# Attention of a hybrid encoder step: the order of 72 heads, and which query tile is prepared when

## The chip, the cores and the metric
The kernel runs on one core of one Trainium2 chip. The metric is the device time of one execution in microseconds (us). A core has five engines: TensorE (PE in the profile, with its weight loads as PEld), VectorE (DVE), ScalarE (ACT), GpSimd (POOL) and SyncE (SP), which here issues DMAs. Each runs its own program in its written order, and they meet through semaphores.

## The reference
One inference step of a one-layer encoder: a gated DeltaNet branch and an MLA attention branch over 1024 prompt rows and 32 sample rows (with 256 cached ones). What concerns the change is the attention, eight heads of 128 (plus 64 rotary) dimensions:

```python
s = einsum('bqhd,bkhd->bhqk', qn, kn) + einsum('bqhd,bkd->bhqk', qr, kr)
s = s.astype(float32) * (QK_HEAD ** -0.5)
mask = (kpos[None, :] // CHUNK) <= (qpos[:, None] // CHUNK)   # CHUNK = 64
s = where(mask, s, -inf)
pr = softmax(s, axis=-1)
return einsum('bhqk,bkhd->bqhd', pr, v)                       # per block of 128 queries
```

qn and qr are the two parts of the projected q, each divided by its root mean square; qr is then rotated by its position. The result, times silu(z_b), goes on to the output projection.

## The kernel before
The kernel has five stages with a meeting of all engines between them (`meet`): the input projections, the latents (keys and values), the attention, the delta rule, and the output branches. The attention is written as one program for each engine, which all loop over the same step number x.

There are nine query tiles of 128 rows: tiles 0 to 7 of the prompt and tile 8, the sample (`NT` is 8). Tile i of the prompt attends 128(i+1) keys, the sample 288. Each has 8 heads, so there are 72 heads, and before the change head x is head x % 8 of tile x // 8. In step x:
- TensorE (`pe_attention`): scores of head x+1 (matmuls at L695 to L697, 512 keys at a time), early jobs, values of head x-1 (L720), transposes of the probabilities of head x (L708), late jobs.
- VectorE (`dve_attention`): maximum of x+1 (`dve_max`, L930 to L934: mask, maximum, scaled and negated), after each fourth head the normalised result `on` (L946, L950), early jobs, the copy of the transposed probabilities beyond 512 keys (L959), late jobs, a step of the decay gate (`dve_decay`) where one is due, a part of the norms of q where one is due.
- ScalarE (`act_attention`): exp of x+1 (L798), early jobs, the copy pT of the first 512 keys of transposed probabilities of x (L814), late jobs, a step of the decay gate.

So every engine is one head ahead with the score side and one behind with the value side. Scores of odd and even heads use two pairs of PSUM banks; there is one bank pair for transposes, one bank for values, and one bank, number 7, for all jobs.

A job is four small transposes through bank 7 (`pe_job`, L681), read by one other engine. The dictionary `jobs` maps a step and a phase (early, late) to its jobs; `order` numbers them, and a job on TensorE waits until all earlier ones were read (`s_r7`). The kinds:
- q, parts 0 to 2: the raw q of a tile (`qraw`, one DMA) turned to rows; ScalarE reads it twice, into `qtok` and squared into `qsq` (L784, L785).
- b, parts 0 and 1: the normalised q turned back, read by ScalarE into `qT` (L787); parts 2 and 3: the rotated part, read by VectorE into `qrT` (L913).
- o: the attended group of four heads turned, multiplied by `zb` into `ub` on VectorE (L922), from where SP stores it.
- d: two jobs of the decay gate for the next stage.

Between q and b lie the norms on VectorE (`dve_q_norms`: part 0 sums and scales, L846 to L850; part 1 the inverse root, eleven small operations at L87 to L98; part 2 the multiply, L858) and the rotation on GpSimd (`pool_attention`, L829 to L839). During the 8 heads of tile i the kernel so prepares tile i+1: norms in its steps 1, 2, 3, b jobs in steps 4, 5, 6, 6, the q jobs of the tile after that in steps 6, 7 and 0 of the next. `qT` and `qrT` have two slots.

SP's program (`sp_attention`) is a single line: q loads, stores of `ub`, loads of `zb`, and, once the prompt's heads are through, the first loads of the delta stage (`sp_load_qkv`, `sp_load_gcum`), whose buffers lie where the attention's keys and values were.

Of the kernel before, what the change touches and what calls it, by code (L numbers as in the profile page):

```python
# [21 lines left out]
P = 128  # L22
# [86 lines left out]
def build(nc, a, o, scr, ctx):  # L109
# [127 lines left out]
    qT = sb(p2b, "qT", [P, 2, H, P])  # L237
    qrT = sb(p2b, "qrT", [P, 2, H, P], F32R)
# [364 lines left out]
    turn = {job: n for n, job in enumerate(order)}  # L603

# [4 lines left out]

    second = [0]  # L610
    for x in range(NX):
        second.append(second[-1] + (len(keys_of(x // H)[2]) > 4))

    def scores_of(x):
        b = 2 * (x % 2)
        return PS[:, b:b + 2].rearrange("p a b -> p (a b)")[:, 0:keys_of(x // H)[1]]

    def load_q(sp, i):
        sp.dma_start(qraw[:, :], scr["proj"][C_Q:C_Q + 12, :, i * P:(i + 1) * P].rearrange("c p n -> p c n")).then_inc(s_qraw, 16)

    def sp_attention(sp):
# [3 lines left out]
        for i in range(NQ):  # L625
            if i == NT - 1:
                sp.wait_ge(s_gT, 1)
                sp.dma_start(scr["gcum"].rearrange("t h n -> (t h) n"), gcT).then_inc(s_so, 16)
            if i + 1 < NQ:
                sp.wait_ge(s_t7, turn[("q", i, 2)] + 1)  # L630
                load_q(sp, i + 1)
            for g in range(2):
                if i:
                    sp.wait_ge(s_r7, turn[("o", 2 * i - 2 + g, 0)] + 1)
                    store_ub(sp, 2 * i - 2 + g)
                sp.dma_start(zb[:, g], scr["proj"][C_ZB + 4 * g:C_ZB + 4 * g + 4, :, i * P:(i + 1) * P].rearrange("c p n -> p c n")).then_inc(s_zb[g], 16)
        sp.wait_ge(s_pv, NT * H)
        sp.wait_ge(s_so, 16)
        for t in range(2):
            sp_load_qkv(sp, t)  # L640
            sp_load_gcum(sp, t)
        for g in range(2):
            sp.wait_ge(s_r7, turn[("o", 2 * NT + g, 0)] + 1)
            store_ub(sp, 2 * NT + g)
        for g in range(2):
            sp.wait_ge(s_us[g], 16 * NQ)

    def store_ub(sp, og):
        i, g = divmod(og, 2)
        sp.dma_start(scr["u"][H + 4 * g:H + 4 * g + 4, :, i * P:(i + 1) * P].rearrange("c p n -> p c n"), ub[:, g]).then_inc(s_us[g], 16)  # L650
# [60 lines left out]
    def pe_values(pe, x):  # L711
        i, h = divmod(x, H)
# [6 lines left out]
        for k, w in enumerate(widths):  # L719
            last = pe.matmul(PS[:, 6, (h % 4) * P:(h % 4 + 1) * P], pT[0:w, x % 2, k], V[0:w, base // P + k, h * HD:(h + 1) * HD],  # L720
# [41 lines left out]
    def act_job(act, job):  # L762
# [23 lines left out]
        else:  # L786
            act.activation(qT[:, i % 2, 4 * part:4 * part + 4].rearrange("p a b -> p (a b)"), PS[:, 7], ACT.Copy, scale=colB[:, B_QN:B_QN + 1]).then_inc(s_r7, 1)  # L787
# [3 lines left out]
    def act_exp(act, x):  # L791
        n = keys_of(x // H)[1]
# [8 lines left out]
    def act_attention(act):  # L801
# [3 lines left out]
        for x in range(NX):  # L805
# [4 lines left out]
            nk = min(4, len(keys_of(x // H)[2]))  # L810
# [9 lines left out]
    def pool_attention(pool):  # L820
        half = ROPE // 2
        for i in range(NQ):
# [4 lines left out]
            cos = rotq[:, i:i + 1, 0].to_broadcast([P, H, ROPE])  # L827
            sin = rotq[:, i:i + 1, 1].to_broadcast([P, H, ROPE])
# [76 lines left out]
    def dve_job(dve, job):  # L905
# [30 lines left out]
    def dve_attention(dve):  # L936
# [3 lines left out]
        for x in range(NX + 2):  # L940
# [12 lines left out]
            if x < NX:  # L953
                nk = len(keys_of(x // H)[2])
# [9 lines left out]
            if 1 <= x % H <= 3 and x // H + 1 < NQ:  # L964
                dve_q_norms(dve, x // H + 1, x % H - 1)
# [125 lines left out]
    def bank(g, b):  # L1091
        return PS[:, 4 * g + b]
# [1240 lines left out]
```

## Time and profile before
| | us |
|---|---|
| median of three runs | 2135.45 (2130.41 to 2136.23) |
| profiled execution | 2133.29, its span 2131.6 |
| of it: TensorE busy | 1984.1 |
| first scores to last transposes of the attention | 294.5 (1173.96 to 1468.50) |

The profile's times count from the start of the span. Busy time of TensorE is that of its matmuls, which overlap each other a little in their pipeline, so that the interval from the start of one group to the start of the next is the better measure of what a group costs. "Idle before" names the operation whose semaphore ended a wait.

### The profile page before, as it was taken

What the parts mean: (1) busy time and instruction counts of PE and PEld (TensorE: products, weight loads), DVE (VectorE), ACT (ScalarE), POOL (GpSimd) and SP (SyncE); (2) the same over time, 40 slices, a digit from 0 to 9 for tenths busy, and PEclk for the clock granted to TensorE, in tenths of its full rate; (3) what the DMA queues carried; (4) which work ended last, traced back from release to release, by engine and by line L of the source; (5) the groups of instructions that cost most, each with busy time, mean ns of one, the idle gap of its engine ahead of it and who ended that gap; (6) DMA issues with size and microseconds to landing.
All of it is one profiled execution on the core that took longest, in us unless ns stands there. A gap on an engine that the chain in (4) does not pass through costs nothing.

```text
span 2131.6 us, 32185 instructions
## 1 busy us (share of the span) xinstructions
PE 1984.1 (93%) x12375; PEld 1818.7 (85%) x12375; DVE 864.0 (41%) x1840; ACT 699.4 (33%) x1528; POOL 199.7 (9%) x248
## 2 busy tenths in 40 slices
PE   6899999999999999987986788998999998999999
PEld 2699999999999999975764567876999997799887
DVE  1545545100100010025642556655676767423332
ACT  2333333211111222213222445434667675211010
POOL 0012212000000000000001221211111010000000
PEclk9899999999999999999998899999999999999999
DMA  9122222322222222132111221115013224523231
GB/s 322 63 95 103 95 95 85 133 95 84 97 112 84 95 99 99 50 101 89 39 29 34 60 70 46 50 30 168 20 62 106 75 79 150 200 74 109 89 115 69
DMA packets 153725, 195.63 MB, mean 92 GB/s; under 512 B 9153, under 2 KB 124910, under 8 KB 153628
## 3 DMA queue, kind: packets, MB, share of 16 engines
q1 hardware_dynamic: 142300, 151.85, 21.1%
q0 software_dynamic: 10064, 38.13, 5.3%
q10 hardware_dynamic: 1264, 4.39, 0.5%
q8 instruction: 57, 0.93, 0.2%
q14 instruction: 40, 0.33, 0.1%
HBM read 134.15 MB, written 60.19 MB: 91 GB/s over the span
## 4 chain that ended last, share of the span: by engine, by line
PE 79%; DVE 8%; ACT 4%; issue 4%; DMA 3%; DVEq 1%; ACTq 0%; POOL 0%; POOLq 0%; SPq 0%
PE PS L2158 40%; PE PS L1468 9%; PE PS L1301 8%; PE PS L1400 4%; PE PS L1473 3%; PE PS L381 3%; PE PS L720 2%; PE PS L695 2%; PE PS L2174 1%; PE PS L681 1%; PE PS L708 1%; DMA Wraw<-in_w_ada 1%; ACT E L1645 1%; DVE amx L932 1%; DVE lst L530 1%
## 5 line engine op out<-in xcount | busy, mean ns | idle before, releaser
L2158 PE MATMUL PS<-HH,WL 128*128 128x352 f32 (+1 forms) x1752 | 379.8, 325 | 5.2 <-DVE mod L2268 5.2
L2158 PE MATMUL PS<-HH,WH 128*128 128x352 f32 (+1 forms) x1752 | 378.4, 323 | 0.0
L2158 PE MATMUL PS<-HL,WH 128*128 128x352 f32 (+1 forms) x1752 | 378.0, 324 | 0.0
L2158 PEld LDWEIGHTS PS<-HH,WL 128*128 128x128 f32 (+1 forms) x1752 | 298.8, 189 | 5.6 <-issue 5.3
L2158 PEld LDWEIGHTS PS<-HH,WH 128*128 128x128 f32 (+1 forms) x1752 | 301.1, 188 | 0.3
L2158 PEld LDWEIGHTS PS<-HL,WH 128*128 128x128 f32 (+1 forms) x1752 | 297.8, 188 | 0.2
L2264 DVE TENSOR_TENSOR WL<-Wraw,WH 128x2048 fp32r<-128x2048 f32 x37 | 84.8, 2293 | 523.1 <-ACT WH L2101 523.1
L2129 ACT ACTIVATE R<-PS 128x1056 f32<-128x1056 f32 x48 | 50.6, 1054 | 409.1 <-PE PS L2158 409.1
L1468 PE MATMUL PS<-WT,QL 128*128 128x128 f32 x832 | 102.5, 277 | 1.2 <-DVE QL L1858 0.9
L720 PE MATMUL PS<-V,pT 128*128 128x128 f32 (+1 forms) x624 | 86.4, 282 | 15.5 <-ACT pT L814 15.3
L1468 PEld LDWEIGHTS PS<-WT,QL 128*128 128x128 f32 x832 | 97.6, 193 | 2.6 <-DVE QL L1858 2.6
L2285 DVE SCALAR_TENSOR_TENSOR R<-R 128x1059 f32<-128x1059 f32 x72 | 95.3, 1323 | 5.4
L720 PEld LDWEIGHTS PS<-V,pT 128*128 128x128 f32 (+1 forms) x624 | 78.0, 193 | 21.5 <-ACT pT L814 19.4
L798 ACT ACTIVATE pr<-PS,amx 128x128 f32<-128x128 f32 (+8 forms) x72 | 51.5, 716 | 135.3 <-DVE amx L934 135.1
L1695 ACT ACTIVATE WT<-PS 128x512 f32<-128x512 f32 x104 | 62.1, 598 | 96.5 <-PE PS L1468 96.5
L381 PE MATMUL PS<-UH,LL 128*128 128x512 f32 x176 | 72.8, 413 | 17.0 <-DVE UL L560 11.0
L695 PE MATMUL PS<-kT,qT 128*128 128x512 f32 (+4 forms) x208 | 85.1, 492 | 1.0 <-DVEq L915 1.0
L1301 PE MATMUL PS<-FH,VL 128*128 128x352 f32 x384 | 84.3, 327 | 0.4 <-DVE FL L1271 0.4
L1301 PE MATMUL PS<-FH,VH 128*128 128x352 f32 x384 | 82.8, 323 | 0.0
L1301 PE MATMUL PS<-FL,VH 128*128 128x352 f32 x384 | 82.6, 323 | 0.0
L1998 POOL DMA_DIRECT2D Wraw<-in_w_in x36 | 31.9, 887 | 504.7 <-DVE WL L2264 432.9
L1858 DVE COPY_PREDICATED QL<-lev,PS 128x512 f32<-128x512 int32 x90 | 60.9, 728 | 36.1 <-PE PS L1473 35.9
(292 smaller groups left out, 3187.5 us busy)
## 6 DMA issues: line engine op xcount, KB each, us to landing
scratch_proj<-R SPq DMA_DIRECT2D x72, 576.0 KB, 2.8
Wraw<-in_w_in POOLq DMA_DIRECT2D x36, 1024.0 KB, 5.5
QKV<-scratch_proj SPq DMA_DIRECT2D x27, 512.0 KB, 5.6
Wraw<-in_w_ada SPq DMA_DIRECT2D x12, 1024.0 KB, 6.0
fr<-scratch_u SPq DMA_DIRECT2D x16, 528.0 KB, 6.6
gr<-scratch_proj SPq DMA_DIRECT2D x16, 528.0 KB, 3.6
qraw<-scratch_proj SPq DMA_DIRECT2D x9, 768.0 KB, 5.1
zb<-scratch_proj SPq DMA_DIRECT2D x18, 256.0 KB, 3.1
```

What stands on the lines that cost most here:

```text
L381: last = pe.matmul(PS[:, bank + half], l[:, slot, r], u[:, j, r, 512 * half:512 * half + 512], start=(r == 0 and begin), stop=(r == KR - 1 ...
L695: pe.matmul(out, qT[:, i % 2, h], kT[:, h, c:c + w], start=True, stop=False)
L720: last = pe.matmul(PS[:, 6, (h % 4) * P:(h % 4 + 1) * P], pT[0:w, x % 2, k], V[0:w, base // P + k, h * HD:(h + 1) * HD], start=(k == 0), s ...
L1301: last = pe.matmul(PS[:, 3 * (n % 2) + b, 0:TB], w[:, l % 2, k, (n % 2) * P:(n % 2) * P + P], u[:, k, b * TB:(b + 1) * TB], start=(k == 0 ...
L1400: last = pe.matmul(PS[:, 4 * slot + h], m[:, slot, k], w[:, k, 512 * h:512 * h + 512], start=(k == 0 and fst), stop=(k == KD - 1 and m is ...
L1468: last = pe.matmul(hs(out, h), lhs(h), rhs(h), start=True, stop=True)
L1473: last = pe.transpose(hs(out, h), src(h), ident)
L1695: act.activation(WT[:, g], bank(g, 3), ACT.Copy).then_inc(d_x, 1)
L1858: x = dve.copy_predicated(heads(QL[:, g, l]), level_mask(l), heads(bank(g, 0)))
L2158: last = pe.matmul(PS[0:m, psum + b, 0:TB], w[:, s, k, c * P:c * P + m], h[:, k, b * TB:(b + 1) * TB], start=(k == 0 and first), stop=(k = ...
L2264: dve.tensor_tensor(WL[:, s], Wraw[:, s], WH[:, s].bitcast(F32), ALU.subtract).then_inc(s_wlo, 1)
L2285: last = dve.scalar_tensor_tensor(cv, x[:, i:i + XW - 3], wt[:, i:i + 1], cv, ALU.mult, ALU.add)
```

## The change
The order of the 72 heads is written out in `order_of_heads`: the 8 heads of tile 3 first; then those of tiles 7, 6, 5, 4, between which, from the fifth on, the heads of tiles 0, 1 and the sample are placed one by one; the last four heads of tile 4 stand alone; tile 2 comes last. From head 12 to head 59 so every even head is one of 640 to 1024 keys, every odd one of 128, 256 or 288.

`PREPARED` is the order in which tiles are prepared: 3, 7, 0, 6, 1, 5, sample, 4, 2. It begins at heads 0, 8, 13, 20, 29, 36, 45, 52, 64 (`begins`). Relative to a tile's first head the preparation lies at fixed steps: the "usual" ones, as before, or the "close" ones, where its first head is less than eight behind that of the tile prepared before. `qT` and `qrT` get four slots. Groups of four heads may now come from two tiles, so `zb` and `ub` are moved with one DMA for each tile in a group (`parts_of`). The last stage of SP's line loads the decay rows of tile 1 after the meeting instead of before it, and the buffers of the delta and output stages move to other addresses (QKV slots rotated by one, E before QKV, VH before fr, the spacer dropped).

```diff
-    qT = sb(p2b, "qT", [P, 2, H, P])
-    qrT = sb(p2b, "qrT", [P, 2, H, P], F32R)
+    NQS = 4
+    qT = sb(p2b, "qT", [P, NQS, H, P])
+    qrT = sb(p2b, "qrT", [P, NQS, H, P], F32R)
...
+    PREPARED = (3, 7, 0, 6, 1, 5, NT, 4, 2)
+    large = [(i, h) for i in (7, 6, 5, 4) for h in range(H)]
+    small = [(i, h) for i in (0, 1, NT) for h in range(H)]
+    order_of_heads = [(3, h) for h in range(H)]
+    for n, head in enumerate(large):
+        order_of_heads.append(head)
+        if 4 <= n < 4 + len(small):
+            order_of_heads.append(small[n - 4])
+    order_of_heads += [(2, h) for h in range(H)]
+    begins = [order_of_heads.index((i, 0)) for i in PREPARED]
...
-    for i in range(NQ):
-        for g in range(2):
-            jobs.setdefault((H * i + 4 * g + 5, EARLY), []).append(("o", 2 * i + g, 0))
-        for step, phase, kind, part in ((-2, LATE, "q", 0), (-1, LATE, "q", 1), (0, LATE, "q", 2), (4, LATE, "b", 0),
-                                        (5, LATE, "b", 1), (6, EARLY, "b", 2), (6, LATE, "b", 3)):
-            if i + 1 < NQ:
-                jobs.setdefault((max(H * i + step, -1), phase), []).append((kind, i + 1, part))
+    norm_steps = {}
+    usual = ((-10, LATE), (-9, LATE), (-8, LATE)), (-7, -6, -5), ((-4, LATE), (-3, LATE), (-2, EARLY), (-2, LATE))
+    close = ((-7, LATE), (-7, LATE), (-6, LATE)), (-5, -5, -4), ((-3, LATE), (-3, LATE), (-2, EARLY), (-2, LATE))
+    for g in range(NX // 4):
+        jobs.setdefault((4 * g + 5, EARLY), []).append(("o", g, 0))
+    for n in range(1, NQ):
+        x = begins[n]
+        turned, normed, back = close if x - begins[n - 1] < H else usual
+        for part, (step, phase) in enumerate(turned):
+            jobs.setdefault((max(x + step, -1), phase), []).append(("q", n, part))
+        for part, step in enumerate(normed):
+            norm_steps.setdefault(x + step, []).append((n, part))
+        for part, (step, phase) in enumerate(back):
+            jobs.setdefault((x + step, phase), []).append(("b", n, part))
...
+        for g in range(NX // 4):
+            if g >= 2:
+                sp.wait_ge(s_r7, turn[("o", g - 2, 0)] + 1)
+                store_ub(sp, g - 2)
+            load_zb(g)
+            while prepared + 1 < NQ and step_of[("q", prepared, 2)] < 4 * g + 4:
+                sp.wait_ge(s_t7, turn[("q", prepared, 2)] + 1)
+                prepared += 1
+                load_q(sp, prepared)
...
+        sp_load_qkv(sp, 0)
+        sp_load_gcum(sp, 0)
+        sp_load_qkv(sp, 1)
...
-            if 1 <= x % H <= 3 and x // H + 1 < NQ:
-                dve_q_norms(dve, x // H + 1, x % H - 1)
+            for n, part in norm_steps.get(x, []):
+                dve_q_norms(dve, n, part)
...
     def sp_delta(sp):
+        sp_load_gcum(sp, 1)
         sp_load_qkv(sp, 2)
```

## Rows read from the trace of the kernel before
**Rows 1.** The page, 40 slices of the span, TensorE's busy tenths.
```profile
PE   6899999999999999987986788998999998999999
```
**Rows 2.** Stages; us, busy of PE, PEld, DVE, ACT, POOL, clock, DMA share, GB/s.
```profile
1173.96:1195.21 21.25, 12.77 (x80) 10.81 (x79) 12.61 (x45) 8.28 (x28) 7.62 (x7) 0.84 0.22 63
...
1274.89:1316.38 41.49, 35.51 (x221) 28.91 (x220) 24.59 (x69) 22.07 (x44) 7.88 (x7) 0.92 0.16 45
...
1394.83:1441.38 46.55, 45.55 (x285) 36.10 (x283) 26.37 (x56) 18.09 (x32) 7.84 (x7) 1.00 0.08 24
1441.38:1468.50 27.12, 24.65 (x156) 20.04 (x156) 9.55 (x25) 9.29 (x25) 0.00 (x0) 0.96 0.60 185
```
**Rows 3.** Timeline, TensorE in tile 7; start, duration, engine, operation.
```profile
1408.42 0.60 PE L681 MATMUL PS<-cst,on 128*128 128x128 f32 x4
1408.85 1.95 PE L720 MATMUL PS<-V,pT 128*128 128x128 f32 x16
1410.64 1.04 PE L708 MATMUL PS<-cst,pr 128*128 128x128 f32 x8
1411.51 1.02 PE L695 MATMUL PS<-kT,qT 128*128 128x512 f32 x2
...
1414.15 1.95 PE L720 MATMUL PS<-V,pT 128*128 128x128 f32 x16
```
**Rows 4.** Waits of TensorE in the attention: total us, times, longest.
```profile
PE PS L720 <- ACT pT L814: 15.3, 13, 2.5
PE PS L681 <- DVE qrT L913: 6.4, 9, 0.8
```
**Rows 5.** Timeline, tile 7: from a head's scores to its exp.
```profile
1424.78 1.95 PE L720 MATMUL PS<-V,pT 128*128 128x128 f32 x16
...
1425.21 1.22 DVE L932 TENSOR_REDUCE amx<-PS 128x1 f32<-128x1024 f32 x1
...
1426.69 1.11 ACT L798 ACTIVATE pr<-PS,amx 128x1024 f32<-128x1024 f32 x1 [2.47 <-DVE amx L934]
```
**Rows 6.** Groups by form in the attention: busy us, mean ns, idle before.
```profile
L932 DVE TENSOR_REDUCE amx<-PS 128x1 f32<-128x768 f32 x8 | 7.7, 958 | 0.6
L814 ACT ACTIVATE pT<-PS 128x128 f32<-128x128 f32 x8 | 2.2, 270 | 1.3 <-PE PS L708 1.3
L858 DVE TENSOR_TENSOR qsq<-qtok,qst 128x1024 f32<-128x1024 f32 x8 | 12.4, 1548 | 0.0
```
**Rows 7.** Timeline of VectorE: norms of q in tile 3, part 2 in tile 4.
```profile
1254.93 1.21 DVE L846 TENSOR_REDUCE qst<-qsq 128x8 f32<-128x1024 f32 x1
...
1258.20 0.17 DVE L87 TENSOR_SCALAR qst<-qst 128x16 int32<-128x16 int32 x1
...
1260.70 0.17 DVE L98 SCALAR_TENSOR_TENSOR qst<-qst 128x16 f32<-128x16 f32 x1
...
1295.08 2.15 DVE L858 TENSOR_TENSOR qsq<-qtok,qst 128x1024 f32<-128x1024 f32 x1
```
**Rows 8.** Timeline of TensorE: a q job right behind another, before tile 0.
```profile
1171.75 0.65 PE L681 MATMUL PS<-cst,qraw 128*128 128x128 f32 x4 [1.18 <-ACT qsq L785]
```
**Rows 9.** Timeline of VectorE: first and last operation of decay step 2.
```profile
1299.45 0.53 DVE L873 TENSOR_SCALAR decay<-decay 128x72 f32<-128x72 f32 x1
...
1303.67 0.07 DVE L894 MEMSET decay<- 64x8 f32 x1
```
**Rows 10.** Timeline of TensorE: end of the attention, start of the delta stage.
```profile
1465.16 1.12 PE L720 MATMUL PS<-V,pT 128*128 128x128 f32 x6 [0.58 <-ACT pT L814]
...
1471.53 1.97 PE L1473 MATMUL PS<-cst,QKV 128*128 128x128 f32 x8 [3.03 <-SPq L306]
```
**Rows 11.** A stretch of ten us in tile 4, columns as in rows 2.
```profile
1295.00:1305.00 10.00, 6.80 (x51) 5.73 (x49) 8.72 (x22) 6.12 (x10) 6.73 (x6) 1.00 0.01 2
```
**Rows 12.** Timeline of TensorE: scores in tile 4 at half clock.
```profile
1308.45 2.01 PE L695 MATMUL PS<-kT,qT 128*128 128x512 f32 x2
```
**Rows 13.** The page, DMA issues: KB each, median us to landing.
```profile
qraw<-scratch_proj SPq DMA_DIRECT2D x9, 768.0 KB, 5.1
```

More of the change, by code:

```diff
@@ L603, in build @@
     turn = {job: n for n, job in enumerate(order)}
+    step_of = {job: when[0] for when in jobs for job in jobs[when]}
     def keys_of(i):
@@ L608, in keys_of, with keys_at, parts_of, load_q @@
         return base, n, [min(P, n - P * k) for k in range(-(-n // P))]
+    def keys_at(x):
+        return keys_of(order_of_heads[x][0])
     second = [0]
     for x in range(NX):
-        second.append(second[-1] + (len(keys_of(x // H)[2]) > 4))
+        second.append(second[-1] + (len(keys_at(x)[2]) > 4))
+    def parts_of(g):
+        found = {}
+        for c in range(4):
+            i, h = order_of_heads[4 * g + c]
+            found.setdefault(i, []).append((c, h))
+        return [(i, slice(v[0][0], v[-1][0] + 1, v[1][0] - v[0][0]), v[0][1], len(v)) for i, v in found.items()]
+    moves = [0, 0]
+    moved = []
+    for g in range(NX // 4):
+        moves[g % 2] += len(parts_of(g))
+        moved.append(moves[g % 2])
     def scores_of(x):
         b = 2 * (x % 2)
-        return PS[:, b:b + 2].rearrange("p a b -> p (a b)")[:, 0:keys_of(x // H)[1]]
-    def load_q(sp, i):
+        return PS[:, b:b + 2].rearrange("p a b -> p (a b)")[:, 0:keys_at(x)[1]]
+    def load_q(sp, n):
+        i = PREPARED[n]
         sp.dma_start(qraw[:, :], scr["proj"][C_Q:C_Q + 12, :, i * P:(i + 1) * P].rearrange("c p n -> p c n")).then_inc(s_qraw, 16)
@@ L637, in sp_attention @@
         sp.wait_ge(s_pv, NT * H)
         sp.wait_ge(s_so, 16)
[L639 to L650, printed above, removed]
+        sp_load_qkv(sp, 0)
@@ L652, in pe_job, with store_ub @@
+        sp_load_gcum(sp, 0)
+        sp_load_qkv(sp, 1)
+        for g in range(NX // 4 - 2, NX // 4):
+            sp.wait_ge(s_r7, turn[("o", g, 0)] + 1)
+            store_ub(sp, g)
+        for b in range(2):
+            sp.wait_ge(s_us[b], 16 * moves[b])
+    def store_ub(sp, g):
+        for i, at, h, n in parts_of(g):
+            sp.dma_start(scr["u"][H + h:H + h + n, :, i * P:(i + 1) * P].rearrange("c p n -> p c n"), ub[:, g % 2, at]).then_inc(s_us[g % 2], 16)
     def pe_job(pe, job):
@@ L694, in pe_scores @@
             out = PS[:, 2 * (x % 2) + b, 0:w]
-            pe.matmul(out, qT[:, i % 2, h], kT[:, h, c:c + w], start=True, stop=False)
-            pe.matmul(out, qrT[:, i % 2, h], krL[:, c:c + w], start=False, stop=False)
-            last = pe.matmul(out, qrT[:, i % 2, h], krH[:, c:c + w], start=False, stop=True)
+            pe.matmul(out, qT[:, slot, h], kT[:, h, c:c + w], start=True, stop=False)
+            pe.matmul(out, qrT[:, slot, h], krL[:, c:c + w], start=False, stop=False)
+            last = pe.matmul(out, qrT[:, slot, h], krH[:, c:c + w], start=False, stop=True)
         last.then_inc(s_sc, 1)
     def pe_transposes(pe, x):
-        widths = keys_of(x // H)[2]
+        widths = keys_at(x)[2]
         pe.wait_ge(s_ex, x + 1)
```

79 lines of the change are left out of this document (39 added, 40 removed).

## The prediction
> **What bounds the kernel now.** Read the page's forty slices first [rows 1]: TensorE is at nine tenths and more nearly everywhere; the exception is slices 18 to 26, and from the 23rd on (53 us a slice) that is the attention, the only part whose order changes. Second, the table by stage [rows 2]: nine rows, one for each query tile, 0 to 7, then the sample; four stand there. From the first scores to the last transposes it is 294.5 us. Tile 0 keeps TensorE busy 12.8 of 21.3 us, tile 7 45.6 of 46.6. Early tiles wait; tiles 5 to 7 hardly do.
>
> How much is wait? A head costs TensorE its scores, values and transposes. From start to start, tile 7 takes 2.64 + 1.79 + 0.87 = 5.30 us, and a job of four small transposes 0.43 to 0.44 [rows 3]. Read the same way at the other widths, the heads of tiles 0 to 7 and the sample cost 0.75, 1.33, 1.98, 2.65, 3.43, 3.98, 4.65, 5.30 and 2.18. Eight of each are 210 us; some 72 jobs 32; the decay jobs 1. So 243 us are work in either order, 51.5 are waits or half clock. By tile (interval less work): 12.1, 10.1, 6.1, 3.9, 9.2, 0.9, 0.5, 0.2, some 8 in the sample and its end. That is all this change can win. Three stretches of half clock lie in tiles 0, 1 and 4 (mean clock 0.84 and 0.92 in two of them [rows 2]), some 5 to 6 us of the 51.5.
>
> Third, the waits [rows 4]: values wait 15.3 us for ScalarE's copy of the transposed probabilities (pT), jobs 6.4 us for VectorE's read of the job before, 0.8 each. These are latencies along a chain, not full engines: VectorE is busy 12.6 of tile 0's 21.3 us [rows 2].
>
> **The chain of a head.** Let t=0 be where TensorE has issued a head's scores. In [rows 5] that is 1424.78; the maximum starts at 1425.21 and takes 1.22, exp starts at 1426.69 and takes 1.11. So exp starts at 0.69+R and ends at 0.69+R+E; R and E, the durations of maximum and exp, shrink with the width (R 0.96 at 768 keys [rows 6]). ScalarE's program has exp of head x+1 before pT of head x. So values of x start 0.74+R(x+1)+E(x+1)+C(x) after the scores of x+1, C being the copy (0.27 for tile 0 [rows 6]). TensorE has only values x-1, transposes x and scores x+2 meanwhile.
>
> **Part 1, pairing.** Let x be small, x+1 large. Tile 7 beside tile 0: the chain needs 0.74+1.22+1.12+0.27 = 3.35, TensorE has 1.78+0.11+0.42 = 2.31: a wait of 1.04 per pair. Likewise 6/0 1.02, 6/1 0.77, 5/1 0.75, 5/sample 0.62, 4/sample 0.56. Alone, a head of tile 0 waits 1.67-0.75 = 0.92, of tile 1 0.69, of the sample 0. The large neighbour's exp stands in front of the small head's copy, so pairing by itself hides nothing here; jobs fill the wait, 0.44 each.
>
> **Part 2, preparation of q.** It costs VectorE 2.25 us (part 0: two reductions, two scalings), 2.8 (part 1, eleven small operations) [rows 7], 1.55 in the mean for part 2 [rows 6] and 2.15 at worst [rows 7], then GpSimd 7.8 busy [rows 2], 8.2 with gaps. Tiles 5 to 7 hide that at 4 to 5 us a head. Where a gap is under eight heads (preparing tiles 0, 6, 5, 4) the change puts parts 0 and 1 in one step, two q jobs back to back, and two b jobs back to back. Jobs share a bank: a second q job sat 1.18 us idle behind the first one's two reads [rows 8], a second b job 0.8.
>
> One case walked through, tile 6's preparation, t=0 at the issued scores of head 16. VectorE: maximum of 16 to 1.9, parts 0 and 1 to 7.05, maximum of 17 to 7.75, `on` to 8.7, second copy of 16 to 9.4, part 2 to 11.55, maximum of 18 to 13.2. TensorE reaches values 16 at 7.1 plus a job and waits until 9.45; transposes 17 end at 11.3, b0 goes at 12.0 after part 2. ScalarE must do exp 18 (to 14.3), copy 17 (14.6), then b0's read (15.3): b1 waits 3 us. Then scores 19, b2 behind b1's read (0.5 more), values 17, transposes 18: 18.3, where the work alone is 11.2. Lost 7.1; with the q pair in head 13 (q1 waits until 4.45; work ends 1.7 earlier) 8.8.
>
> The same walk elsewhere. Tile 5's (heads 29 to 34, pairs 6/1): q pair 1.7; values 32 wait 2.6 for the second copy, b1 3.0, b2 0.9, a reload of exp's table 0.6: 6.9 after what would fill: 8.6. Tile 4's (45 to 50, 5/sample): 1.6 + 5.8 = 7.4. Tile 0's (heads 6 to 11, tile 7 alone): values 9 wait 1.7, b1 3.0: 4.7. The roomy ones, parts a step apart: tile 1's 5.0 (values 23 wait 1.5, values 25 2.4, the rest bare waits); the sample's, together with the decay gate, 8.6: step 2 of the decay holds VectorE 4.3 us without a break [rows 9], maximum 38 is late 3.4, and the decay job behind a q job waits for ScalarE 3.4; tile 2's 3.0. The b3-q0 adjacency of 0.8 in every tile now stays only once; the walks have that.
>
> Here a rule of the notes can be weighed. Part 2 took 2.15 us in [rows 7], beside GpSimd; its usual is shorter. The Trainium skill (GPSIMD Engine Reference, opening table) says that GpSimd's SBUF interface is shared with VectorE, with contention for VectorE instructions with two SBUF inputs; part 2 has two. By that rule every compressed case collides, as walked; without it each is 0.6 to 0.9 shorter, the sum about 3 us less, on the same side.
>
> **Part 3, the ends.** Tile 3 first: its own 3.9 stays, a longer first chain adds 0.9 (0.69+0.69+0.69+0.14 = 2.2, one head's scores of 1.32 meanwhile), q1 behind q0 behind b3 1.3: 6.1. Tile 4's last four heads alone 1.0. Tile 2 last: chain 2.37 against 1.98, 0.39 a head less two jobs: 2.3; the drain 1.4+0.7+1.1 = 3.2 (now 0.6+0.6+1.1, the first of them in [rows 10]): 5.5. Pairs with no preparation (19, 51, 53, 55): 1.4.
>
> SP: a mixed group moves zb and ub in two DMAs instead of one, 0.4 to 0.5 us of SP each; their readers come four heads later. The q loads stand in SP's order behind stores of groups that end earlier: 0 while that holds. Delta's start: the decay rows of tile 1 and QKV 2 are issued after the meeting, QKV 2 1.5 us later; neither is read in the first 15 us of that stage, so 0, at worst 1.5. The wait of 3.0 us there [rows 10], for the last store, stays; one load fewer ahead of it could give back up to 1.5. Taken: 0.
>
> **Sum.** 6.1 + 4.7 + 8.8 + 8.6 + 7.4 + 5.0 + 8.6 + 3.0 + 1.4 + 1.0 + 5.5 = 60.1 us of waits at full clock. Half clock: in the ten us before it fell in tile 4, TensorE was busy 6.8 [rows 11]; the walks have 60 to 70% at four places. At half clock the two matmuls of [rows 12] took 2.01 instead of 1.02 [rows 3], so a stretch of 6.8 us, three quarters busy, costs 2.5. I take two, between none and five: 5. After 65.1, before 51.5: +13.6. On the profiled execution's own 2133.3 (span 2131.6 and 1.7 around it) that is 2146.9. The median of three runs, 2135.45, is 2.2 higher, inside their spread; I say 2147.
>
> The Trainium skill (TensorE: Matmul & The Clock Gate, the table of two states) has 1.2 GHz as the idle state and 2.4 GHz as the busy one, which speaks for mixing thin tiles with thick ones. The trace agrees so far as the low means stand in tiles 0, 1 and 4. By it alone, all half clock gone, the sum would be 5 less and come out at 2142.
>
> **Rivals.**
> Hidden: VectorE works ahead during the large head's scores, and a preparation costs what it does in tiles 5 to 7, under 1 us. Then bare pair waits net of jobs 8.5, adjacencies 4 x 2.1, decay 2.5, start 5, tile 7 alone 1, ends 6: 31.4, full clock: -20, 2113 (2106 to 2126). For it: tiles 5 to 7. Against: it decides whether parts 0 and 1, 5.1 us, fit between two maxima, and in a pair VectorE has about 2 us before the next small one. 0.18.
> Half hidden: waits absorb each other, 51 to 54 in all: 2137, give or take 5. 0.22.
> [...] 0.12.
> Late load: a q load behind a store keeps a q job waiting up to its 5.1 us from issue to landing [rows 13], at head 35 or 45: 2150. 0.04.
> Not as it says: too few slots, so that preparation waits for heads still to come. By the order a slot's last head is over at least fourteen heads before it is written: 0.02, some 2150.
> My forecast, 2140 to 2156: 0.42.
>
> **Chances.** 0.3% is 6.4 us, about what a measurement of this kernel can tell from no change: faster below 2129, slower above 2142. Faster: the hidden case and 0.03 of the half case, 0.21. Same: the rest of the half case and the low edge of mine, 0.21. Slower 0.58. The range, 2120 to 2160, cuts most of the hidden case and the top of the clock case.
>
> **What would show it.** Values of small heads waiting about 1 us for pT where no job stands; the second b job waiting over 2 us for ScalarE's read, four times; VectorE's run of eleven small operations right ahead of a maximum that TensorE then waits for; half clock behind these. Wrong if heads 12 to 60 have TensorE over 93% busy, or if first scores to last transposes is under 290 us (forecast 308), or if the tail of tile 2 shows no waits for pT.

## The result, and the profile after

The changed kernel takes 2150.7 us (median of four runs, three of which lie at 2150.4 to 2150.9) beside 2133.3 for the kernel before: ratio 1.0077, 95% interval 1.0058 to 1.0097. Timed again in the first experiment (run a1_after) it takes 2144.5 (2142.3 to 2147.5) beside 2132.3: ratio 1.0063 (1.0039 to 1.0087). The change makes the kernel slower by 12 to 17 us; the forecast was 2147, +13.6. The fourth run of the first set, 2846.6 us at a mean clock of 0.65, fell in a slower state and was the profiled one, so every view of after here is that of a1_after (2142.7 us, span 2141.1).

The page of after, TensorE's busy tenths in forty slices:

```profile
PE   6899999999999999978886887888999998999999
```

Against [rows 1] seven slices differ, each by a tenth: 18 to 20, ahead of the attention, and 23, 25, 26 and 27 in it. The page alone doesn't show where the time went. First scores to last transposes take 309.9 us (1170.57 to 1480.51) instead of 294.5: +15.4. What stands before that stretch took 3.4 us less in this execution, and what stands behind it 2.5 less. Such differences lie between one execution and the next: in the profiles below the attention starts between 1169.8 and 1176.6.

By stage, columns as in [rows 2]; the rows are heads 12 to 19, 28 to 35, 36 to 43, 52 to 59 (all pairs), and 64 to 71 (tile 2):

```profile
1223.22:1266.74 43.52, 35.06 (x224) 28.29 (x223) 22.26 (x55) 15.15 (x33) 7.82 (x7) 0.96 0.15 43
...
1295.79:1336.04 40.25, 31.93 (x200) 26.09 (x198) 21.93 (x57) 17.88 (x40) 8.03 (x8) 0.96 0.18 53
1336.04:1372.11 36.07, 28.20 (x180) 24.19 (x181) 20.59 (x64) 17.01 (x42) 7.81 (x7) 0.95 0.18 52
...
1411.70:1437.44 25.74, 25.46 (x166) 20.86 (x167) 12.15 (x32) 11.46 (x27) 0.00 (x0) 1.00 0.12 34
...
1455.80:1480.51 24.71, 21.59 (x141) 17.57 (x141) 10.74 (x33) 9.11 (x25) 0.00 (x0) 0.99 0.60 181
```

Read the fourth row against those above it. In the pairs of heads 52 to 59 (tile 4 with the sample) TensorE is busy 25.46 of 25.74 us. Of a preparation they hold only tile 2's three q jobs, one a head (1424.14, 1427.78 and 1430.79), and part 0 of its norms (1435.02); GpSimd's column is 0.00, as its rotation comes later. Pairs with the rest of a preparation have TensorE busy 31.93 of 40.25 and 28.20 of 36.07. So pairs of these widths cost next to nothing by themselves or with parts so far apart, and what is done for later tiles in the pairs above costs much. For the narrowest heads, tile 0's, no such stretch exists; where no job stood, one of them waited 0.89 (below, at 1249.32).

Less the work that both orders hold (243 us by the prediction, 242.6 before rounding), the stretches have these microseconds of waits and half clock (half clock: TensorE at a granted clock of 0.50, 1.2 instead of 2.4 GHz):

| heads | measured | forecast |
|---|---|---|
| 0 to 7: tile 3 | 6.1 | 6.1 |
| 8 to 19: tile 7, preparation of 0 and 6 | 15.6 | 13.9 |
| 20 to 27: of tile 1 | 4.1 | 5.0 |
| 28 to 35: of tile 5 | 11.8 | 8.6 |
| 36 to 43: of the sample, decay | 10.5 | 8.6 |
| 44 to 51: of tile 4 | 10.9 | 7.8 |
| 52 to 63: of tile 2, and the last heads of tile 4 | 3.6 | 4.7 |
| 64 to 71: tile 2, end | 4.7 | 5.5 |
| sum | 67.3 | 60.1 at full clock + 5 |

In the third column the bare pair waits (1.4 for heads 19, 51, 53, 55) stand with the stretches they lie in, 0.35 each. The 5 us of half clock stand in no stretch of that column; the measured column holds them.

The waits of TensorE in the attention, as in [rows 4]: total, times, longest:

```profile
PE PS L770 <- ACT pT L864: 10.9, 14, 1.5
PE PS L729 <- DVE ub L973: 9.6, 6, 2.3
PE PS L729 <- ACT qsq L835: 6.8, 5, 2.1
PE PS L745 <- DVEq L966: 6.2, 7, 1.0
PE PS L729 <- DVE on L1002: 5.9, 4, 1.6
PE PS L729 <- ACT qT L837: 4.4, 6, 1.5
```

Before, the one large line was values for pT, 15.3. That line fell to 10.9, so a part of the chain was hidden as the order intends. In its place stand 26.7 us of L729, which is `pe_job`: b jobs that wait for VectorE's `ub`, jobs behind q jobs for ScalarE's two reads, o jobs for `on`, jobs behind b jobs for `qT`. The same four were 6.9 us before (2.7, 2.3, 1.1 and 0.8), of which the largest two:

```profile
PE PS L681 <- DVE ub L922: 2.7, 3, 2.3
PE PS L681 <- ACT qsq L785: 2.3, 5, 0.7
```

And the scores (L745) now wait seven times 0.9 for VectorE's read of the last b job, which scores did once before (1.0) and jobs nine times (6.4).

The place that the prediction walked through, tile 6's preparation, with t=0 at 1245.98. Lines picked from the timeline of all engines, in order of time (others lie between them); in brackets the idle time before and what ended it:

```profile
1247.78 1.21 DVE L897 TENSOR_REDUCE qst<-qsq 128x8 f32<-128x1024 f32 x1
...
1249.32 0.49 PE L770 MATMUL PS<-V,pT 128*128 128x128 f32 x2 [0.89 <-ACT pT L864]
...
1253.38 0.29 DVE L984 TENSOR_REDUCE amx<-PS 128x1 f32<-128x128 f32 x1
...
1254.06 0.69 DVE L1002 TENSOR_TENSOR on<-PS,ari 128x512 f32<-128x512 f32 x1
1254.66 0.68 DVE L1011 COPY pT<-PS 128x512 f32<-128x512 f32 x1
1254.89 0.63 PE L729 MATMUL PS<-cst,on 128*128 128x128 f32 x4 [1.56 <-DVE on L1002]
1255.26 1.48 DVE L909 TENSOR_TENSOR qsq<-qtok,qst 128x1024 f32<-128x1024 f32 x1
1255.45 2.02 PE L770 MATMUL PS<-V,pT 128*128 128x128 f32 x16
...
1256.94 1.22 DVE L984 TENSOR_REDUCE amx<-PS 128x1 f32<-128x1024 f32 x1
...
1258.37 0.69 DVE L973 TENSOR_TENSOR ub<-PS,zb 128x512 f32<-128x512 f32 x1
1259.12 0.66 PE L729 MATMUL PS<-cst,qsq 128*128 128x128 f32 x4 [1.54 <-DVE ub L973]
...
1260.56 0.65 PE L729 MATMUL PS<-cst,qsq 128*128 128x128 f32 x4 [0.78 <-ACT qT L837]
...
1266.63 1.13 PE L745 MATMUL PS<-kT,qT 128*128 128x512 f32 x2 [1.00 <-DVEq L966]
```

VectorE goes from 1247.78 to 1253.0 through parts 0 and 1 of the norms, and head 17's small maximum, which takes 0.29, stands behind them. The prediction has VectorE's maximum 17 done at t=7.75, `on` at 8.7, the second copy at 9.4 and values 16 at 9.45. The rows have `on` over at 8.8, the copy at 9.4 and values 16 at 9.47.

### The profile page after: what moved, and what is told of

Read it like the earlier page. It is cut to its first block, busy times and chain, and to the rows that moved or that the text cites. A ratio compares the mean times of both kernels' runs of the same rounds, so it can differ in the third digit from the quotient of the medians.

```text
span 2844.9 us, 32227 instructions
## 1 busy us (share of the span) xinstructions
PE 2750.8 (97%) x12375; PEld 2272.5 (80%) x12375; DVE 867.7 (30%) x1840; ACT 702.4 (25%) x1528; POOL 199.8 (7%) x248
## 4 chain that ended last, share of the span: by engine, by line
PE 92%; DVE 3%; issue 2%; DMA 2%; ACT 1%; DVEq 1%; ACTq 0%; SPq 0%
PE PS L2211 41%; PE PS L1521 11%; PE PS L1353 9%; PE PS L381 6%; PE PS L1452 5%; PE PS L1526 4%; PE PS L770 3%; PE PS L745 3%; PE PS L2227 2%; PE PS L729 2%; PE PS L758 2%; PE PS L302 1%; DMA Wraw<-in_w_ada 1%; PE PS L747 1%; PE PS L746 1%
## 5 line engine op out<-in xcount | busy, mean ns | idle before, releaser
L2211 PE MATMUL PS<-HH,WL 128*128 128x352 f32 (+1 forms) x1752 | 498.8, 405 | 5.2 <-DVE mod L2321 5.2
L2211 PE MATMUL PS<-HH,WH 128*128 128x352 f32 (+1 forms) x1752 | 498.6, 405 | 0.0
L2211 PE MATMUL PS<-HL,WH 128*128 128x352 f32 (+1 forms) x1752 | 498.4, 404 | 0.0
L2211 PEld LDWEIGHTS PS<-HH,WL 128*128 128x128 f32 (+1 forms) x1752 | 353.0, 206 | 49.5 <-issue 5.3
L2211 PEld LDWEIGHTS PS<-HH,WH 128*128 128x128 f32 (+1 forms) x1752 | 352.8, 206 | 44.3
L2211 PEld LDWEIGHTS PS<-HL,WH 128*128 128x128 f32 (+1 forms) x1752 | 352.9, 206 | 44.0
L1521 PE MATMUL PS<-WT,QL 128*128 128x128 f32 x832 | 145.7, 349 | 0.6 <-DVE QL L1911 0.6
L1521 PEld LDWEIGHTS PS<-WT,QL 128*128 128x128 f32 x832 | 140.9, 256 | 1.6 <-DVE QL L1911 1.3
L745 PE MATMUL PS<-kT,qT 128*128 128x512 f32 (+4 forms) x208 | 119.6, 667 | 5.9 <-DVEq L966 5.9
L848 ACT ACTIVATE pr<-PS,amx 128x896 f32<-128x896 f32 (+5 forms) x72 | 51.4, 714 | 203.4 <-DVE amx L986 203.4
L381 PE MATMUL PS<-UH,LH 128*128 128x512 f32 x176 | 90.2, 513 | 0.0
```

The costliest lines, as they stand in the source:

```text
L381: last = pe.matmul(PS[:, bank + half], l[:, slot, r], u[:, j, r, 512 * half:512 * half + 512], start=(r == 0 and begin), stop=(r == KR - 1 ...
L745: pe.matmul(out, qT[:, slot, h], kT[:, h, c:c + w], start=True, stop=False)
L1521: last = pe.matmul(hs(out, h), lhs(h), rhs(h), start=True, stop=True)
L2211: last = pe.matmul(PS[0:m, psum + b, 0:TB], w[:, s, k, c * P:c * P + m], h[:, k, b * TB:(b + 1) * TB], start=(k == 0 and first), stop=(k = ...
```

## The experiments

Each kernel was timed beside the kernel before on the same chip. "Attention" is first scores to last transposes in its profile, and "at half" how long in it TensorE's granted clock was 0.50; before has 294.5 and 22.4. (In b1, b2, b3, b4, c1 and c3 the first matmul of the stretch began at half clock, and its 0.1 to 0.4 us over the usual are not counted.)

| run | what | median, us | ratio to before, 95% | attention, us | at half, us |
|---|---|---|---|---|---|
| a1_after | the change | 2144.5 | 1.0063, 1.0039 to 1.0087 | 309.9 | 14.1 |
| a2_roomy | closely placed preparation of three tiles spread | 2134.4 | 1.0014, 1.0002 to 1.0026 | 302.3 | 17.1 |
| a3_sequence | whole tiles in the new order of preparation | 2127.3 | 0.9980, 0.9970 to 0.9990 | 293.2 | 20.5 |
| a4_copy_first | ScalarE's copy ahead of the exp | 2151.0 | 1.0083, 1.0055 to 1.0111 | 314.7 | 27.3 |
| b1_no_norms_after | the change, no norms on VectorE | 2120.8 | 0.9941, 0.9920 to 0.9961 | 285.4 | 3.9 |
| b2_no_norms_before | before, no norms | 2113.2 | 0.9904, 0.9887 to 0.9920 | 275.9 | 6.2 |
| c1_no_norms_sequence | a3, no norms | 2113.3 | 0.9909, 0.9892 to 0.9927 | 277.3 | 7.7 |
| b3_sequence_decay | a3, decay gate beside tile 7 | 2125.9 | 0.9966, 0.9947 to 0.9985 | 293.8 | 30.9 |
| c3_sequence_decay | the same again | 2123.5 | 0.9955, 0.9941 to 0.9969 | 293.7 | 30.9 |
| b4_ahead | b3, preparation early | 2134.3 | 1.0000, 0.9989 to 1.0012 | 298.2 | 11.4 |
| c2_ahead_spread | b3, early and spread | 2130.8 | 0.9992, 0.9983 to 1.0001 | 293.8 | 10.2 |

**a1_after: the change as it is.** The views above are its own.

> The changed kernel again, for a profile. Theory (waits of the walks): 2150; first scores to last transposes about 308 us; VectorE's parts 0 and 1 in one step followed by a wait of values of about 2 us, and a second b job waiting about 3 us, at heads 8 to 11, 15 to 18, 31 to 34, 47 to 50; small heads without a job wait about 1 us for pT. Rival (the pairs hide everything, the loss lies outside the attention): attention under 290 us and a longer delta stage.

309.9 us where 308 was forecast. The stretches agree within 3.2 us each, and the places of the losses are those that were named. What TensorE waits for there was foreseen only in part: values in the first close place wait 1.44 and a small head without a job 0.89, as said, but the second b jobs wait 1.46, 0.78, 0.78 and 0.78 instead of about 3.

**a2_roomy: the close placing of parts taken away where it can be.** Only tile 0's preparation stays close; those of tiles 6, 5 and 4 get the usual steps.

```diff
-        turned, normed, back = close if x - begins[n - 1] < H else usual
+        turned, normed, back = close if x - begins[n - 1] < H - 1 else usual
```

> The close spacing only for the preparation of tile 0; those of tiles 6, 5 and 4 get the usual steps. Theory: the compressed preparations cost 24.8 us of waits, as roomy ones some 15 and a q job right behind a b job more: 5 to 10 us faster than the changed kernel, 2140 to 2145. Rival (the interleaving itself costs, not where the norms stand): within 2 us of 2150. Rival (clock): over 12 us faster, since no place is left that lowers it.

It gives back 7.6 us of attention (309.9 to 302.3) and 10 us in the medians, the upper end of what was expected of the difference; the 2134.4 itself lies under the 2140 to 2145. The waits of its TensorE:

```profile
PE PS L770 <- ACT pT L864: 16.4, 16, 2.7
...
PE PS L729 <- DVE ub L973: 4.1, 3, 2.3
...
PE PS L729 <- DVE on L1002: 1.1, 1, 1.1
```

The waits of jobs for `ub` and `on` fell from 15.5 to 5.2, those of values for pT rose from 10.9 to 16.4. Putting two parts in one step is thus about half of the loss of 15.4, but spreading them shifts a part of it back to the chain. The interleaved order without it still isn't faster than before.

**a3_sequence: the other half of the change, without interleaving.** All heads of a tile together; PREPARED is also the order of the tiles, tile 3 first and tile 2 last, and the slots and SP's order stay as changed.

```diff
-    PREPARED = (3, 7, 0, 6, 1, 5, NT, 4, 2)
-    large = [(i, h) for i in (7, 6, 5, 4) for h in range(H)]
...
+    PREPARED = (3, 7, 6, 5, 4, 0, 1, NT, 2)
+    order_of_heads = [(i, h) for i in PREPARED for h in range(H)]
```

> Everything of the change but the interleaving: tiles whole, in the order 3, 7, 6, 5, 4, 0, 1, sample, 2, all preparations usual, four slots, new buffers, new order on SP. Theory: by the waits of each tile in the trace of before (4.8, 0.2, 0.5, 0.9, 9.2, 12.1, 10.1, 3, 5.5) 46 us instead of 51.5: 2127 to 2132, some 20 faster than the changed kernel. Rival (the loss is in SP's line, the buffers or the end of the stage): 2145 or more. Rival (interleaving gains and the preparations lose): 2135 to 2145.

2127.3, ratio 0.9980: slots, buffers, starting with tile 3 and ending with tile 2 cost nothing, and the whole loss is in the interleaving, 16.8 us of attention (309.9 - 293.2). The DMAs split over two tiles come with the interleaving and aren't in a3; in a1's attention no wait of TensorE, VectorE or ScalarE ends with a DMA of SP, so they aren't seen to cost anything either. The 50.6 us that its heads wait lie at tiles 3, 7, 6, 5, 4, 0, 1, sample, 2 as 4.7, 1.2, 1.0, 1.8, 8.8, 12.1, 10.6, 5.8, 4.6. Tiles 7, 4 and 0 in the table by stage:

```profile
1196.50:1241.83 45.33, 44.38 (x274) 34.93 (x273) 26.27 (x55) 18.07 (x32) 7.83 (x7) 1.00 0.14 41
...
1322.68:1363.79 41.11, 35.26 (x232) 28.95 (x231) 24.75 (x70) 21.95 (x44) 7.89 (x7) 0.96 0.16 46
1363.79:1388.66 24.87, 16.72 (x115) 14.65 (x114) 14.51 (x50) 10.81 (x36) 7.63 (x7) 0.86 0.26 75
```

**a4_copy_first: is it ScalarE's order in a pair?** The prediction's part 1 says that the large head's exp stands in front of the small head's copy. Here the copy goes first in the pairs.

```diff
+            first = x % 2 == 1 and 13 <= x <= 59
-            if x + 1 < NX:
+            if x + 1 < NX and not first:
                 act_exp(act, x + 1)
...
+            if first:
+                act_exp(act, x + 1)
```

> In odd steps 13 to 59 ScalarE copies pT of the small head before exp of the large one. Theory: the copy then waits for transposes of the small head and holds exp back, and transposes of the large head wait about 1 us instead of the values of the small one: 2147 to 2154, no real gain. Rival (the wait for pT is all there is): 24 pairs lose 0.6 to 1 us less, 2135 to 2140.

The wait for pT falls from 10.9 to 4.7, and the kernel wins nothing by it, as expected: 2151.0, attention 314.7 us. In their place stand other waits:

```profile
PE PS L729 <- ACT qsq L835: 8.5, 5, 2.3
...
PE PS L729 <- DVE on L1005: 7.6, 5, 2.3
...
PE PS L770 <- ACT pT L865: 4.7, 6, 1.4
PE PS L758 <- ACT pr L848: 3.2, 6, 0.7
```

ScalarE's timeline shows how. The large head's maximum is over at 1251.03, but its exp now stands behind the small head's transposes and copy and starts at 1251.41, and TensorE's transposes wait for the exp (L758, 3.2 us in six waits):

```profile
1251.24 0.28 ACT L865 ACTIVATE pT<-PS 128x128 f32<-128x128 f32 x1 [3.40 <-PE PS L758]
...
1251.41 1.11 ACT L848 ACTIVATE pr<-PS,amx 128x1024 f32<-128x1024 f32 x1
```

The order on ScalarE only chooses which of the two heads is late. That a4's attention is longer than a1's by 4.7 us shows no more: its profile has TensorE at half clock for 27.3 us, busy 23.8 of them, a1's for 14.1, busy 13.0, and half of the difference between the busy times, 5.4, is more than the 4.7.

**b1, b2, c1: how much of the loss is VectorE's norms of q?** In these three, VectorE leaves out the norms of q for all tiles but the first prepared (sums, inverse root, multiply); waits and signals stay. The same edit is made in after, before and a3:

```diff
 def dve_q_norms(dve, i, part):
+        if i:
+            if part == 0:
+                dve.wait_ge(s_r7, turn[("q", i, 2)] + 1)
+            elif part == 1:
+                dve.wait_ge(s_qrr, i)
+                dve.drain().then_inc(s_qr, 1)
+            else:
+                dve.drain().then_inc(s_qn, 1)
+            return
```

> The changed kernel with VectorE's norm operations (parts 0, 1, 2 of q) left out for all tiles but the first prepared, waits and semaphores kept; q is then not normalised. Theory (VectorE's 6.5 us per preparation, put into pairs, is the loss): first scores to last transposes falls from 309.9 to 285 us, each of the stretches around heads 16 to 20, 32 to 36, 48 to 52 from 8 or 9 us of waits to about 3. Rival (the interleaving itself, its chains and job pairs, is the loss): falls by no more than the kernel before does without them, to 295 or more.

> The kernel before with the same operations left out; q is then not normalised. Theory: it gains in tiles 0 to 3 only, 294.5 to about 279 us, so that the two orders are about 6 us apart instead of 15. Rival: they stay 12 us or more apart.

> The whole tiles of a3 with VectorE's norm operations left out as in b1 and b2; q is then not normalised. It splits the 9.6 us that b1 and b2 still lie apart. Theory A (what is left is the interleaving's own: job pairs back to back, scores waiting for the last b job's read, bare waits of the pairs): first scores to last transposes 274 to 277 us, as the kernel before without them. Theory B (what is left comes with the order of the tiles, the slots or the buffers): 282 us or more.

q is then not normalised; these kernels are there for their times alone. The whole attention of c1, then of b1, columns as in [rows 2] (b2's, read the same way, takes 275.86 us):

```profile
1174.89:1452.20 277.31, 255.19 (x1646) 208.51 (x1644) 125.51 (x324) 129.32 (x292) 54.74 (x56) 0.99 0.23 66
```

```profile
1170.67:1456.12 285.45, 256.04 (x1645) 206.97 (x1643) 125.31 (x324) 129.07 (x292) 54.74 (x56) 0.99 0.22 65
```

Leaving the norms out wins 24.5 us in the interleaved order (309.94 to 285.45), 15.8 in the sequence (293.15 to 277.31) and 18.7 before. So of the 16.8 us between interleaved and sequence, 8.7 (24.49 - 15.84) are norms that hit pairs harder than whole tiles, and 8.1 (285.45 - 277.31) remain without any norm. b1's own 285 was expected; b1 against b2 is 9.6, between the two expectations (6, and 12 or more). c1's 277.3 is close to the 274 to 277 of its theory A and far from the 282 of B: what remains is the interleaving's own. Half clock doesn't make these differences: it falls by 10.2 us from a1 to b1 and by 12.8 from a3 to c1, and b1 has less of it than c1.

Most of the 8.1 can be followed in the waits: all of TensorE's in the attention are 28.2 us in b1 and 21.5 in c1. b1's largest:

```profile
PE PS L729 <- ACT qsq L835: 6.8, 5, 2.1
PE PS L770 <- ACT pT L864: 6.3, 11, 1.2
PE PS L745 <- DVEq L975: 6.2, 7, 1.0
PE PS L729 <- ACT qT L837: 3.7, 5, 1.0
```

and the lines of c1 that answer to them (the b job's read by VectorE is waited for by the next job there, L722, and not by the scores):

```profile
PE PS L722 <- DVE qrT L966: 6.1, 8, 0.9
PE PS L763 <- ACT pT L857: 3.8, 6, 1.2
PE PS L722 <- DVE ub L975: 2.5, 2, 2.1
PE PS L722 <- ACT qsq L828: 2.5, 5, 0.9
...
PE PS L722 <- ACT qT L830: 1.3, 2, 0.7
```

The jobs behind q jobs wait 4.3 us more in pairs (6.8 against 2.5), values 2.5 more, b jobs behind b jobs 2.4 more; VectorE's read costs the same in both (6.2, 6.1), and jobs wait for `ub` 1.9 less in pairs (0.6 against 2.5). The growth is the two q jobs and the two b jobs in one phase, and the bare chain of a pair. b1's first pair shows the last by itself, at 1245.52: values wait 0.89, as at 1249.32 in a1, where the walk had 1.04.

**b3, c3: a version that beats both.** In a3, tile 4 loses 8.8 us, where the decay gate runs (`XD` still points at heads 32 on). Moved beside tile 7, where a head takes 5.3 us:

```diff
-    XD = H * (NT // 2)
+    XD = H
```

> The whole tiles of a3 with the decay gate's steps at heads 8 to 17 (tile 7) instead of 32 to 41 (tile 4). Theory: the 8.8 us of waits of tile 4 fall to about 2, tile 7 takes 1 to 2 more: 5 to 6 us faster than a3, 2121 to 2123. Rival (the decay was not the cause of tile 4's waits, its narrow heads were): within 1.5 us of a3.

> b3 again beside c2, to tell them and the kernel before apart: 2126, 4 to 8 us under the kernel before. If b3's gain over a3 (1.4 us of the 6 expected) was eaten by half clock in tiles 0 and 1, its profile again has 25 us or more of half clock between first scores and last transposes; if that was chance, under 20.

2125.9 and 2123.5, in the second set beside 2131.7 of before: faster than the kernel before by 0.45% (0.31 to 0.59%). The 2121 to 2123 expected of b3 were missed: it is 1.4 us under a3 by the medians, which was the rival's sign. The stages speak against the rival all the same. Tiles 7, 4 and 0 in c3's profile:

```profile
1199.69:1248.03 48.34, 45.33 (x278) 35.40 (x277) 29.51 (x69) 24.59 (x44) 7.83 (x7) 1.00 0.14 39
1328.66:1363.28 34.62, 32.78 (x228) 27.51 (x227) 21.04 (x56) 15.32 (x32) 7.82 (x7) 1.00 0.19 54
1363.28:1389.63 26.35, 18.20 (x117) 15.97 (x115) 14.40 (x49) 10.56 (x33) 7.61 (x7) 0.78 0.25 72
```

Tile 4 shrinks by 6.5 us (41.11 to 34.62), of which a stretch of 3.4 us at half clock in a3's is at most 1.7; tile 7 grows by 3.0, tile 0 by 1.5 at clock 0.78 instead of 0.86. The attention of this one execution, 293.7, is no shorter than a3's. Of the two cases named beforehand for c3's profile it is the first, 25 us of half clock or more: 30.9, as in b3's, where a3's has 20.5. It is also the slowest of its six, 2131.1; the other five are 2119.9 to 2123.7. What sets them apart is in the next section.

**b4, c2: preparation far ahead.** With four slots a tile can be prepared long before its turn. Up to the sample's or tile 1's, b4 starts a preparation every six heads, c2 every seven with the b jobs a head apart. The two kernels' lines are shown together; the comments say whose a line is:

```diff
+    starts = (None, -2, 4, 10, 16, 22, 28, 34, 54)       # b4
+    starts = (None, -2, 5, 12, 19, 26, 33, 46, 54)       # c2
...
-        x = begins[n]
+        x = starts[n]
+        for part in range(3):
+            jobs.setdefault((max(x + part, -1), LATE), []).append(("q", n, part))
+            norm_steps.setdefault(x + 3 + part, []).append((n, part))
...
```

> As b3, with each preparation begun early, six heads apart from head 4 on, so that those of tiles 0, 1 and the sample lie beside tiles 6 to 4, and tiles 0 and 1 host none (tile 2's stays beside the sample). Theory: tile 0's waits fall from 12.1 to 6.5 us (the bare chain, 0.92 a head, less two jobs), tile 1's from 10.6 to 4.8, the wide tiles take 2 to 4 more: 2111 to 2116. Rival (narrow heads wait for their own chain whoever is prepared beside them): within 3 us of b3.

> Whole tiles, decay at heads 8 to 17, preparations of tiles 6 to 1 seven heads apart from head 5 on with their jobs in separate steps (b at +6 late, +7, +8, +9 early), so that tile 0 hosts hardly anything; the sample's stays beside tile 1, tile 2's beside the sample. Theory (b4's wide tiles lost 21 us because its first b job stood ahead of the norm it needs and its jobs stood back to back): wide tiles as in b3, tile 0's waits 13.6 to 7: 2119 to 2123. Rival (early preparation costs the wide tiles as much as it saves): 2127 or more.

Both miss what was expected of them (2111 to 2116, and 2119 to 2123) by 7 us and more; c2 lies where its rival had it. The thin tiles get faster: tile 1 takes 14.7 us in b4 (1409.54 to 1424.20), with three jobs in it, instead of c3's 25.1 with nine; tile 0 takes 20.2 in c2 (1372.87 to 1393.11) instead of 26.4. The jobs that lie elsewhere are 2.6 us of the first difference and 0.9 of the second, and a part is clock: 1.00 against 0.82, and 0.92 against 0.78. The wide ones take it back; in b4 the first b job of each tile, in the early phase, waits for VectorE's multiply:

```profile
PE PS L719 <- DVE qsq L899: 9.4, 8, 2.4
```

c2 moves that job back, and the b jobs then wait for `ub` of the group's o job instead:

```profile
PE PS L721 <- DVE ub L965: 8.5, 6, 2.2
```

Neither beats c3. That a better placing within a head would keep both gains is plausible, and wasn't tried.

## Why the prediction was right, and where it wasn't

**The sign and the size.** 309.9 us of attention against 308 forecast, 294.5 before. The likeliest case (pairs lose what their preparation takes, because TensorE finds no cover beside a small head) is shown by a1's stretches, by a2 and by b1 against c1, for about half of the loss; the other half is job pairs and bare chains, which the walks had as well. The rival "hidden" (2113) needed TensorE over 93% busy in heads 12 to 59; it was busy 178.4 of 214.2 us, 83%. Heads 52 to 59 reach 99%, and there, for q jobs a head apart and one part of the norms, that rival is right.

**The start, the end, SP.** Tile 3 as first 6.1 against 6.1. Tile 2 as last 4.7 against 5.5. Its last values wait 1.20 and 0.58 for pT and the last job 1.13, 2.9 of the 3.2 forecast for that drain. SP taken at 0: the meeting's wait is 3.04, as before [rows 10], TensorE waits for no other load in the delta stage, and VectorE's one wait for SP, 2.3 us, is there in both orders:

```profile
1483.55 1.33 PE L1526 MATMUL PS<-cst,QKV 128*128 128x128 f32 x5 [3.04 <-SPq L306]
```

**The steps that failed inside a sum that held.**
- "b1 waits 3 us", in each of the four close places. The second b job waited 1.46 in the first of them and 0.78 in the others. There the first one waited instead, 1.54, 2.21 and 1.72, for VectorE's `ub` of the group before: an operation that the walk had left out of VectorE's order. It stands behind maximum 18, so job b0, next in bank 7 behind the o job, can't start before it is read. In the place walked through, b0 went at t=13.1 instead of 12.0 and b1 at 14.6 instead of 15.4. The transposes of 18 were then over at 19.0 instead of 18.3, because from 15.6 on TensorE was at half clock, busy 3.0 of 3.4 us, which is some 1.5 us more than at full clock. So b1's 2.2 us too many met 1.1 too few ahead of b0 and the half clock: that the walk's end nearly fits is luck.
- Part 2 of the norms was walked with 2.15 us, the longest of [rows 7], and took 1.48 here; its mean over the attention was 1.60, before 1.55 [rows 6].
- "The b3-q0 adjacency of 0.8 in every tile now stays only once." The q job is gone from behind b3, but the scores that now stand there wait for the same read: 7 times, 6.2 us. Before it was 6.4, 9 times [rows 4], in front of jobs. A wait moved was booked as a wait saved, some 5 us in all.
- The q pairs were priced at 1.6 to 1.8 with what stands behind them. The second q job waits 1.17 or 1.18, as in [rows 8]; the o job behind a pair in the decay stretch, which no walk has, 2.10.
- The stretches of tile 5, the sample and tile 4 lost 33.2 us where 25.0 were forecast. They hold four of the waits of scores behind b3, 3.4 us in all, and three stretches of half clock, busy 9.5 us in all, some 4.8 us by half of that: together the 8.2, if the walks' other errors cancelled, which no run takes apart.

**Half clock.** The prediction took 5 us for after and 5 to 6 for before, so no change. In the profiles TensorE ran at half clock for 14.1 us of a1's attention, busy 13.0 of them, and for 22.4 of before's, busy 17.2. By half of the busy time that is an estimate of 6.5 us at most for after and 8.6 for before. Taken off the measured 67.3, the 6.5 leave 60.8 beside the 60.1 of the sum at full clock. One of four such stretches, with the ten us ahead of it:

```profile
1336.90:1346.90 10.00, 7.90 (x53) 6.76 (x51) 5.48 (x21) 7.10 (x13) 0.00 (x0) 1.00 0.01 2
1346.90:1350.30 3.40, 3.40 (x16) 3.40 (x17) 1.87 (x4) 0.99 (x2) 0.00 (x0) 0.51 0.00 0
```

The first row is at 2.4 GHz, and its last 2.10 us TensorE stood still ahead of an o job; the second is at 1.2 GHz. All four are as long (a fifth reaches 0.45 us into the attention's end). They lie at three of the four close places and at the decay step, and each begins within 3 us of a job's wait of 1.5 to 2.2 us; waits of 1.57 (ended 1293.42) and 2.33 (ended 1368.33) have none behind them, so the wait alone doesn't decide it. The Trainium skill has the busy state as the one at 2.4 GHz (TensorE: Matmul & The Clock Gate, the table of two states in Part 1). The trace of after agrees in direction, 14.1 us at half clock against 22.4 with the thin heads apart, and not with the prediction's estimate that by this rule all of it would go.

How much is this in time? All runs of one kernel line up by their mean granted clock. Before, 50 runs: 2136.5 at 0.968 or 0.969, 2134.0 at 0.970, 2131.1 at 0.973, 2129.7 at 0.974: about 1.2 us for each 0.001. Compared at 0.974, by a line through each kernel's runs:

| | us at a mean clock of 0.974 |
|---|---|
| before (50 runs) | 2129.8 |
| the change (4) | 2146.7 |
| a2 (10) | 2137.4 |
| a3 (10) | 2128.6 |
| a4 (4) | 2148.3 |
| b3 and c3 (11) | 2125.6 |
| b4 (10) | 2136.5 |

By the scatter of the runs about them, the lines of a2, a4 and b4 leave about 1 us of doubt each way, the others less. At equal clock the change costs 16.9 us; its median in the second timing shows 12.2, as its runs there have 0.974 to 0.977 and those of before 0.968 to 0.974. So in that timing some 4 us of its cost are given back by the clock. In the first timing it ran at 0.972 to 0.973, and the medians are 17 us apart. Of a3's gain of 5 us most is clock as well (1.2 at equal clock); of c3's 8, about half. c3's profiled execution ran at 0.970, its others at 0.975 to 0.978: why that profile shows no shorter attention.

**What stays open.** Whether the places of jobs alone (one q or b job a head, as in heads 52 to 59, with the norms as they are) would bring the interleaved order below before: a2 goes a part of that way and stops at 1.0014, with tile 0's preparation still close. And what decides, from execution to execution, how many half-clock stretches a kernel gets wasn't seen.

## What to carry to other kernels

Before mixing small work with large work to hide the latency of the small, ask what else hides beside the large: here the preparation of the next tiles, which whole large tiles cover for 1 to 2 us (a3, tiles 7, 6 and 5). Stretches of eight heads in pairs lose 4 us with such a preparation at its usual steps (tile 1's) and 11 to 12 where it is close, bare waits and 1.5 to 1.6 us of half clock included. Walk one such place with every operation of every engine in its program's order, the ones of another group too, and when a wait disappears, look at what now stands in its place behind the same event. Compare kernels at equal mean clock before a difference of a few us is explained by their order.

## What the runs showed of the hardware

- One kernel's executions on one core differ by up to 11 us (c3, 2119.9 to 2131.1), and the mean granted clock orders them, 0.978 to 0.970.
- Stretches of half clock in a1's attention last 3.4 us, half of the 6.8 that the forecast took for one after those of before; c3's are 6.8 again.
- VectorE's multiply of 128x1024 takes 1.22 us at the least and 2.05 at most in a1, mean 1.60. The Trainium skill (GPSIMD Engine Reference, section 1, Specifications) names the SBUF interface shared with GpSimd as a cause for such an instruction with two SBUF inputs, and the trace agrees. In the seven of nine where a GpSimd operation was under way as the multiply began, it took 1.07 to 1.08 us plus their overlap (0.36 to 0.97 us: 1.44 to 2.05); in the other two, where it ended within 0.08 us or began behind the multiply, 1.22 and 1.23 (GpSimd's spans are the roughest of the profile). GpSimd's own next operation, of 128x256, then took 1.70 to 1.72 us instead of 0.71 to 0.73. Beside the multiply at 1255.26 (1.48, of which 0.41 with the GpSimd operation before), and just behind it:

```profile
1255.62 1.72 POOL L883 TENSOR_TENSOR qrx<-qrr,rotq 128x256 f32<-128x256 f32 x1
...
1257.30 0.71 POOL L884 TENSOR_TENSOR qrx<-qrr,rotq 128x256 f32<-128x256 f32 x1
```
